# Computing the even steps' score products right behind the odd steps' value products in a neighbourhood attention

## The reference

```python
def neighbourhood_attention(q, k, v, rpb):
    ...
    scores = jnp.einsum('bhrnqd,bhrnikd->bhrnqik', q_blk, kg).astype(jnp.float32)
    bias = rpb.astype(jnp.float32)[:, d_row[:, None, None, :, None], d_col[None, :, :, None, :]]
    scores = scores + bias[None]
    scores = jnp.where(valid[:, :, None, :], scores, -1e30)
    probs = jax.nn.softmax(scores, axis=(-2, -1)).astype(v.dtype)
    out = jnp.einsum('bhrnqik,bhrnikd->bhrnqd', probs, vg)
```

## Time and profile before

| | |
|---|---|
| median of 3 runs | 2751.53 us (2751.48 to 2751.84) |
| profiled execution, its own time | 2751.87 us |
| its span, first to last instruction | 2750.1 us |
| TensorE busy | 2742.6 us, 100% |
| VectorE, ScalarE, GpSimd busy | 1925.0, 1389.3, 108.3 us |
| granted TensorE clock | 1.00 in the whole span |
| block 2's attention, first scores to last scores | 1436.84 to 1628.4 us |

### The profile page before, as it was taken

One profiled execution on the slowest core, in us unless ns is written; L12 is line 12 of the kernel. 1 busy time (PEld: TensorE's weight loads), 2 busy tenths in 40 slices (PEclk: granted clock), 3 DMA queues, 4 the chain that ended last, 5 costly groups with the idle time before them and its releaser, 6 DMA issues.

```text
span 2750.1 us, 35028 instructions
## 1 busy us (share of the span) xinstructions
PE 2742.6 (100%) x13140; PEld 2243.0 (82%) x13140; DVE 1925.0 (70%) x2769; ACT 1389.3 (51%) x2240; POOL 108.3 (4%) x105
## 2 busy tenths in 40 slices
PE   9999999999999999999999999999999999999999
PEld 8888877788888888888887778888888888888887
DVE  7877566765866667688956653889546866666796
ACT  7332566424645544454446551888424655544454
POOL 0000112000000000000003320000000000000000
PEclk9999999999999999999999999999999999999999
DMA  4333433433334385451352121112223343385541
GB/s 161 114 116 108 168 108 108 145 104 142 144 148 153 142 303 194 157 157 35 138 179 62 55 74 49 55 57 60 83 77 142 137 151 153 138 330 164 157 153 66
DMA packets 102486, 356.58 MB, mean 130 GB/s; under 512 B 10800, under 2 KB 10928, under 8 KB 96176
## 3 DMA queue, kind: packets, MB, share of 16 engines
q1 hardware_dynamic: 100880, 349.37, 36.4%
q10 hardware_dynamic: 1440, 4.98, 0.6%
HBM read 251.54 MB, written 102.76 MB: 129 GB/s over the span
## 4 chain that ended last, share of the span: by engine, by line
PE 99%; DVE 1%; ACT 0%; issue 0%; POOL 0%; DVEq 0%; ACTq 0%; POOLq 0%
PE ps L523 17%; PE ps L3485 12%; PE pa L3877 11%; PE ps L3877 11%; PE ps L3906 9%; PE pa L3906 9%; PE pa L3522 6%; PE ps L3522 6%; PE pa L523 4%; PE ps L3792 2%; PE pa L3613 2%; PE ps L3994 2%; PE ps L3926 2%; PE pa L3658 2%; PE pa L3624 1%; PE pa L3636 1%
## 5 line engine op out<-in xcount | busy, mean ns | idle before, releaser
L1786 ACT ACTIVATE krh<-k_rraw 128x512 fp32r<-128x512 f32 x192 | 121.1, 631 | 255.6 <-PE ps L3906 116.5
L513 DVE TENSOR_TENSOR w_lo<-w_raw,w_hi 128x1024 fp32r<-128x1024 f32 (+1 forms) x100 | 119.6, 1196 | 140.7 <-ACT w_hi L507 140.6
L2882 DVE TENSOR_TENSOR krl<-k_rraw,krh 128x512 fp32r<-128x512 f32 x192 | 132.8, 692 | 117.8 <-ACT krh L1786 117.6
L507 ACT ACTIVATE w_hi<-w_raw 128x1024 fp32r<-128x1024 f32 (+1 forms) x100 | 101.7, 1018 | 196.7 <-PE ps L523 112.3
L523 PE MATMUL ps<-a_hi,w_hi 128*128 128x512 f32 x576 | 177.5, 389 | 0.0
L523 PE MATMUL ps<-a_lo,w_hi 128*128 128x512 f32 x576 | 177.4, 389 | 0.0
L523 PE MATMUL ps<-a_hi,w_lo 128*128 128x512 f32 x576 | 177.4, 389 | 0.0
L3877 PE MATMUL pa<-xh,fwh 128*128 128x512 f32 x448 | 174.5, 390 | 0.0
L3877 PE MATMUL ps<-xh,fwh 128*128 128x512 f32 x448 | 174.4, 389 | 0.0
L3877 PE MATMUL ps<-xh,fwl 128*128 128x512 f32 x448 | 174.4, 389 | 0.0
L3877 PE MATMUL pa<-xl,fwh 128*128 128x512 f32 x448 | 174.4, 389 | 0.0
(11 more groups left out here) (500 smaller groups left out, 6790.3 us busy)
## 6 DMA issues: line engine op xcount, KB each, us to landing
w_raw<-wstream SPq DMA_DIRECT2D x100, 512.0 KB, 3.6
k_rraw<-hff SPq DMA_DIRECT2D x192, 256.0 KB, 2.7
hff<-hbuf SPq DMA_DIRECT2D x32, 1024.0 KB, 3.9
wA<-wff SPq DMA_DIRECT2D x16, 2048.0 KB, 7.6
hff<-hbuf SPq DMA_DIRECT2D x32, 768.0 KB, 3.2
w_raw<-wff SPq DMA_DIRECT2D x32, 512.0 KB, 4.4
f_raw<-wff SPq DMA_DIRECT2D x32, 512.0 KB, 4.4
proj<-res SPq DMA_DIRECT2D x24, 512.0 KB, 5.9
```

What stands on the lines that cost most here:

```text
L507: nc.scalar.activation(w_hi[:, slot, 0:n], w_raw[:, slot, 0:n], ACT.Copy).then_inc(s_whi, 1)
L513: nc.vector.tensor_tensor(w_lo[:, slot, 0:n], w_raw[:, slot, 0:n], w_hi[:, slot, 0:n].bitcast(F32), ALU.subtract).then_inc(s_wlo, 1)
L1786: nc.scalar.activation(k_r[e % 4][0][:], k_rraw[:, e % 4], ACT.Copy).then_inc(sem("s_khi"), 1)
L2882: nc.vector.tensor_tensor(k_r[e % 4][1][:], k_rraw[:, e % 4], k_r[e % 4][0][:].bitcast(F32), ALU.subtract).then_inc(sem("s_klo"), 1)
```

## The change

The scores of step s + 1 are issued in the odd step s, right behind its values, in place of at the start of step s + 1. This holds for even steps from 4 to 30, except 24: 13 steps. All else keeps its order, on VectorE and ScalarE too.

```diff
+        def scored_ahead(s):
+
+            return 4 <= s < N_PAIR2 * STEPS_PER_PAIR and s % 2 == 0 and s != 3 * STEPS_PER_PAIR
+
...
-                    if s < ns:
+                    if s < ns and not scored_ahead(s):
                         scores(2 * s)
                     if s >= 3 and s % 2:
                         values(2 * (s - 3))
                         values(2 * (s - 2))
+                        if scored_ahead(s + 1):
+                            scores(2 * (s + 1))
                     if p + 1 < npair and V_STEP[2] <= q < V_STEP[2] + VB[2]:
                         pe.wait_ge(s_pt, j0 + 2 * (s - 1))
                         v_batch(VB[2] * (p + 1) + q - V_STEP[2])
```

## The result

| | before | changed |
|---|---|---|
| median of 20 runs, us | 2751.75 (2751.04 to 2752.15) | 2756.34 (2755.76 to 2757.01) |
| span of the profiled execution, us | 2750.1 | 2754.2 |
| ratio | | 1.0016, 95% interval 1.001 to 1.0023 |

The change makes the kernel 4.6 us slower. The forecast was +3.4 us, 2754.9, with 2751.2 to 2758.0 as its range; "no change within 0.2%" held too, as 4.6 us is 0.17%.

A forecast was written before the change was run, and what follows sets the result against it. TensorE's starts were taken to bound the kernel. The terms 1.0 + 1.9 + 0.7 + 0.3 - 0.5 = +3.4 us on 2751.87 gave 2755.3 profiled; the median, 0.34 lower, was forecast at 2754.9 us, range 2751.2 to 2758.0.

The forecast's parts named there:

- no change within 0.2%: Whole kernel: the time differs by less than about 5.5 us, what a measurement can tell; chance 0.81.
- the border: TensorE's changes between product shapes: 0.93 us removed from the even step, 0.73 added in the odd, -0.20 us a step.
- The 0.73 us behind the values: Odd step on TensorE: six score products behind the values take the same 0.73 us as in the even step.
- The new wait: Odd step: the second head's score product waits for VectorE's second sum, all of it lost, +0.28 us a step.
- The net +0.08 a step: Each moved step: 0.73 + 0.28 - 0.93 us together, +1.0 us over 13 steps.
- v_out: Steps 6, 14 and 20: transposes wait for ScalarE's delayed v_out; +1.9 us for 6 and 14, +0.7 for 20.
- Step 25: VectorE does a weight unit first, so its first sum is late and the new wait grows by +0.3 us.
- steps 26, 28 and 30 gain 0.17 each: Second transposes no longer wait for ScalarE's copy behind a late exponential, as scores come a step earlier; -0.5 us together.
- Step 29: VectorE's sums late behind a weight unit, but step 28's exponentials and the unit come earlier, so nothing was counted.
- ScalarE hides it: Rival: v_out isn't late, because ScalarE catches up between two copies; +0.8 us, 2752.3 us, chance 0.17.
- The broken pairs cost more: Rival: a product running alone makes the second head's wait 0.45 us a step; +6.1 us, 2757.6 us, chance 0.15.
- Borders alone count: Rival: both new waits are absorbed, by the staggering and by ScalarE; -3.1 us, 2748.4 us, chance 0.08.

The follow-up runs named there:

- the sums first: Changed kernel, but in odd steps VectorE makes both heads' sums before both maxima; 2751.71 us against 2751.64 for the kernel before, ratio 1.0.
- the dose: Changed kernel, with VectorE repeating the first head's maximum in odd steps, delaying the second sum; 2762.32 us against 2751.63 for the kernel before, ratio 1.0039.

## Why the prediction was right, and where it was off

- **The bound and the border.** TensorE's starts carried all of it. The 0.73 us behind the values, an assumption in the prediction, is the 0.73 seen with the sums first, and a moved step without waits gains 0.15 to 0.20 us.
- **The new wait.** Forecast 0.28 us with all of it lost, measured 0.30. The net +0.08 a step measured 0.06 to 0.16 in the seven pairs that have nothing else: 0.81 us in all instead of 0.56. The bounds that the range took for it, -0.05 to +0.25, don't follow from the terms: -0.20 + 0.10 is -0.10, and both upper ends together are -0.08 + 0.45 = +0.37. The measured values lie inside either way.
- **v_out.** The pairs 5/6, 13/14 and 19/20 were forecast at 1.01, 1.01 and 0.78 us and measured 1.00, 1.05 and 0.79. Leaving these steps out took 2.9 us away.
- **Step 25.** Its late sums and step 26's gain were forecast at +0.18 us with the step's own 0.08, measured +0.13.
- **What failed** is the step "steps 26, 28 and 30 gain 0.17 each". It holds for 26 and 30. For 28 "that exponential is long done" was wrong, since `a2_lo` stands ahead of the sums: the pair measured +0.67 instead of -0.09, and where no gap was forecast the second transposes come 0.98 us after the last fill, the 0.23 of the stream included. I had listed `a2_lo` in VectorE's order and not moved it along with the rest by the 1.01 us, and it had only 0.29 us to spare. Here lies 0.76 of the 1.26 us between forecast and stage. Step 29, counted at nothing because step 28's work would come earlier, stayed late for the same reason, as step 28's trace has it: ScalarE goes from the late exponential to the weight unit's high half without a pause, and VectorE's low half starts 0.78 us before step 29's values, as before the change (0.77). Step 29's transposes come 1.29 us later where others come 1.02, and its pair has 0.25 more. The seven pairs above make up the other quarter microsecond.
- **The rivals.** "ScalarE hides it" fell with step 6's rows. "The broken pairs cost more" fell by the dose: 0.76 us late, 0.75 lost. Its price had the same double count of the v_out places as my expectation for the dose; without it, it would have been 5.6. "Borders alone count" is what the rule on mode changes in the Trainium skill ("TensorEngine Tiling (Array Packing)", "Key Properties") comes to here: it gave the gain's sign, and no run reached it until the waits were taken away one by one.

## What to carry to other kernels

When work moves forward on the engine that sets the time, price the border that it saves, then follow each buffer that it now needs sooner to the engine that frees it. That engine's list, in its fixed order, decides the price, and two instructions exchanged there (here two sums ahead of two maxima) can be worth more than the move. The work behind the moved piece comes later by its full length: shift every chain that hangs on it, look where such a chain ends in a wait that was near zero, and check again after each repair, because one wait hides the next.

## What I had not expected of the hardware

When two products share the array, one in each half of its rows, a late second one costs just its own lateness. A second head that starts 0.30, 0.46 or 0.76 us late makes the visit longer by 0.30, 0.46 and 0.75 us. From its load to the next fill the time is again that of an unhindered visit: 1483.43 - 1482.70 = 0.73 us in step 7, 1485.51 - 1484.79 = 0.72 with the dose. The first head doesn't run ahead. In these traces the reason can be the order of the list as well as the array: the two heads' products alternate, so the first head's second product stands behind the second head's first, and it starts 3 ns behind it in step 7 and 4 ns with the dose. No run issues all three products of the first head before the wait, so whether that would absorb a part of it isn't shown.
